# Hybrid encoder layer: last expert's down projection by quarters of its columns, second part of the last norm on TensorE for three tiles

## What is computed

```python
def expert_choice_moe(x, w_router, w_gate, w_up, w_down):
    ...
    gates, idx = lax.top_k(jnp.swapaxes(affinity, 1, 2), cap)      # cap = 64 tokens for each expert
    xe = jax.vmap(lambda xb, ib: xb[ib])(x, idx)
    hid = jax.nn.silu(xe @ w_gate) * (xe @ w_up)                   # 64 x 2048, for each expert
    ye = (hid @ w_down) * gates                                    # 64 x 1024
    # ye's rows are added to the rows idx of a (512, 1024) array of zeros
x = layer_norm(DN_ALPHA * x + expert_choice_moe(x, ...), ln3_g, ln3_b)
```

## Time and profile before

| what | us |
|---|---|
| median of 3 runs | 1263.48 (1261.69 to 1265.07) |
| the profiled execution | 1265.04 |
| its span in the profile | 1263.2 |
| TensorE busy in the span | 1171.1 (93%) |
| VectorE, ScalarE, GpSimd busy | 269.1, 192.6, 138.5 |
| read from memory | 442.02 MB, 352 GB/s over the span |
| mean granted clock of TensorE | 0.984 |

### The profile page before, as it was taken

The page is one execution under the profiler, slowest core; times in us unless marked ns, Lnnn a source line. Parts: engine busy times, 40 slices in busy tenths (PEclk is TensorE's granted clock), DMA queues, the critical chain, the costliest instruction groups (busy, mean ns, idle before and its releaser), DMA issues.

```text
span 1263.2 us, 13663 instructions
## 1 busy us (share of the span) xinstructions
PE 1171.1 (93%) x5804; PEld 590.9 (47%) x5804; DVE 269.1 (21%) x491; ACT 192.6 (15%) x348; POOL 138.5 (11%) x67
## 2 busy tenths in 40 slices
PE   8999998999999999998899889978997998899995
PEld 6887776888743433442243324323432432243321
DVE  2032377727700010010001000200110020002114
ACT  4244434143000000010000001000000000000002
POOL 4454335330000200000000000000000000000002
PEclk9999999999999999999999999999999999899998
DMA  9432213149789999999999999999999999999995
GB/s 361 183 134 83 93 67 126 40 196 386 283 309 428 433 410 431 426 436 432 432 432 432 432 432 432 432 432 431 432 432 432 432 432 432 432 423 427 429 425 210
DMA packets 28644, 444.65 MB, mean 352 GB/s; under 512 B 4544, under 2 KB 4928, under 8 KB 10304
## 3 DMA queue, kind: packets, MB, share of 16 engines
q1 hardware_dynamic: 26304, 441.89, 83.1%
q10 hardware_dynamic: 2304, 2.24, 0.5%
HBM read 442.02 MB, written 2.10 MB: 352 GB/s over the span
## 4 chain that ended last, share of the span: by engine, by line
PE 65%; DMA 28%; DVE 4%; ACT 1%; issue 1%; POOL 0%; SPq 0%; DVEq 0%; ACTq 0%; POOLq 0%
DMA ring<-in_w_exp 27%; PE bank L1293 18%; PE bank L1338 15%; PE bank L1166 5%; PE bank L1255 4%; PE bank L811 2%; PE bank L813 2%; PE bank L816 2%; PE bank L1225 1%; PE bank L989 1%; PE bank L991 1%; PE bank L990 1%; PE bank L1322 1%; DVE yt L1384 1%; PE bank L800 1%
## 5 line engine op out<-in xcount | busy, mean ns | idle before, releaser
L1293 PE MATMUL bank<-ring,yt 128*64 128x512 f32 x2000 | 451.8, 605 | 45.5 <-DMA ring<-in_w_exp 45.4
L1293 PEld LDWEIGHTS bank<-ring,yt 128*64 128x64 f32 x2000 | 145.8, 139 | 340.3 <-issue 293.1
L1338 PE MATMUL bank<-ring,yt 128*64 128x512 f32 x944 | 212.6, 603 | 21.5 <-DMA ring<-in_w_exp 16.6
L1338 PEld LDWEIGHTS bank<-ring,yt 128*64 128x64 f32 x944 | 67.8, 138 | 145.3 <-issue 128.8
L1685 DVE TENSOR_TENSOR work<-bank,work 128x512 f32<-128x512 f32 x32 | 22.1, 692 | 379.2 <-PE bank L1293 379.2
L761 ACT ACTIVATE work<-bank 128x512 f32<-128x512 f32 x32 | 19.1, 597 | 502.3 <-PE bank L1293 502.3
L547 POOL TENSOR_TENSOR stat<-stat 128x1 f32<-128x1 f32 x4 | 2.2, 553 | 831.3 <-DVE stat L1718 831.1
L532 POOL TENSOR_TENSOR piece<-ring,piece 128x1024 fp32r<-128x1024 f32 x31 | 74.7, 2410 | 97.8 <-ACT piece L598 97.8
L1696 DVE TENSOR_TENSOR xT<-bank,xT 128x512 f32<-128x512 f32 x56 | 38.8, 692 | 137.1 <-PE bank L1255 137.1
L1166 PE MATMUL bank<-yt,res 128*128 128x128 f32 x512 | 60.6, 277 | 0.0
L1166 PEld LDWEIGHTS bank<-yt,res 128*128 128x128 f32 x512 | 59.3, 194 | 0.8 <-issue 0.8
(11 more groups left out here) (247 smaller groups left out, 1083.5 us busy)
## 6 DMA issues: line engine op xcount, KB each, us to landing
ring<-in_w_exp SPq DMA_DIRECT2D x66, 4096.0 KB, 29.9
ring<-in_w_exp SPq DMA_DIRECT2D x39, 2048.0 KB, 28.6
ring<-in_dense SPq DMA_DIRECT2D x12, 2048.0 KB, 7.8
ring<-in_w_exp SPq DMA_DIRECT2D x6, 3072.0 KB, 29.1
ring<-in_w_exp SPq DMA_DIRECT2D x14, 1024.0 KB, 28.0
ring<-in_x_turned SPq DMA_DIRECT2D x8, 256.0 KB, 6.9
res<-in_na_bias SPq DMA_DIRECT2D x1, 2048.0 KB, 24.0
res<-in_x SPq DMA_DIRECT2D x1, 2048.0 KB, 7.8
```

Source lines behind the costliest of these rows:

```text
L1293: mm = nc.tensor.matmul(bank[2 * g + n % 2][64 * c:64 * c + 64, :], xeT[:, kk, 64 * e:64 * e + 64], exp_rhs(j, first, k, c), start=kk == 0 ...
L1338: mm = nc.tensor.matmul(bank[5][64 * n:64 * n + 64, :], hidT[:, s, 64 * c:64 * c + 64], exp_rhs(j, first, s, n), start=(g, c, s) == (0, 0, ...
```

## The change

The last expert's down weights are laid out otherwise by the host: chunk 20 + q holds quarter `q` (256 columns) of all 2048 hidden channels, in place of a quarter of the hidden channels for all columns. So each quarter of the output is finished with its chunk. Even and odd blocks of hidden channels go to the two partition halves and are summed by the scatter, whose matrix has the expert in both halves. ScalarE copies each finished quarter; TensorE scatters quarters 0 to 2 to banks 6 and 7 while the next chunks run, and VectorE adds them to `y_acc` and takes their statistics. Of the identity products only that of the last quarter is left. The last quarter is added in banks 0 and 1; VectorE takes its statistics, and does the gain of all four tiles in the order 0, 1, 2, 3. For tiles 0, 1 and 2 the second part of the norm is done by TensorE, with a matmul by a diagonal matrix of the inverse deviations (`scaler`, made by ScalarE) added to a product of a row of ones and the bias row; ScalarE copies the result to SBUF. Tile 3's is done by VectorE. GpSimd has only the four powers. The stores go in the order 0, 1, 2, 3.

```diff
+QUARTERS, QUARTER = 4, D // 4
+QUARTER_BANK = (5, 2, 3, 5)
+TURNED_TILES = (0, 1, 2)
+TURNED_BANKS = (3, 1, 2)
...
-            for n, t in enumerate(STORE_ORDER):
-                sp.wait_ge(normed, 2 * TT + n + 1)
+            for t in range(TT):
+                sp.wait_ge(finished[t], 2 if t in TURNED_TILES else 1)
                 sp.dma_start(out[0, P * t:P * t + P, :], y_acc[:, t, :]).then_inc(stored, 16)
...
+            for q in range(QUARTERS):
+                act.wait_ge(exp_used, LAST * CPP + (CPE + 8 + q + 1))
+                if q >= 2:
+                    act.wait_ge(last_mixed, TT + 2 * (q - 2) + 2)
+                nc.scalar.activation(y_quarter[q % 2], bank[QUARTER_BANK[q]][:, 0:QUARTER], ACT.Copy).then_inc(last_ye, 1)
+            def finish(n):
+                t = TURNED_TILES[n]
+                for a in range(2):
+                    act.wait_ge(tile_scaled, 2 * n + a + 1)
+                    nc.scalar.activation(y_acc[:, t, 512 * a:512 * a + 512], two[TURNED_BANKS[n]][:, a, :], ACT.Copy)\
+                        .then_inc(finished[t], 1)
+            for n, t in enumerate(TURNED_TILES):
+                act.wait_ge(last_rstd[t], 1)
+                nc.scalar.activation(scaler[n], ident, ACT.Copy, scale=rstd(t)).then_inc(scaler_ready, 1)
+                if n:
+                    finish(n - 1)
+            finish(len(TURNED_TILES) - 1)
...
+            def quarter_scatter(q):
+                pe.wait_ge(last_ye, 2 + q)
+                for t in range(TT):
+                    b, final = t // 2, q == QUARTERS - 1
+                    if t % 2 == 0 and not final:
+                        pe.wait_ge(last_kept, 2 * TT + (2 * (q - 1) + b + 1 if q else 0))
+                    mm = nc.tensor.matmul(in_bank(b if final else 6 + b)[:, t % 2, :], last_scat[1][:, t, :], y_quarter[q % 2],
+                                          start=not final, stop=not final or t % 2 == 1)
+                    if t % 2:
+                        mm.then_inc(tile_done if final else last_mixed, 1)
+            def quarter_down(q, ms):
+                j = CPE + 8 + q
+                for m in ms:
...
+                    for s in range(4):
+                        n = s % 2
+                        mm = nc.tensor.matmul(bank[QUARTER_BANK[q]][64 * n:64 * n + 64, 0:QUARTER],
+                                              last_hidT[m // 2][:, s, 64 * (m % 2):64 * (m % 2) + 64],
+                                              exp_chunk(j, False)[:, m, QUARTER * s:QUARTER * s + QUARTER],
+                                              start=m == 0 and s < 2, stop=m == 3 and s >= 2)
...
             def last_down():
-                turn_hid(0)
-                start_tile(1)
-                pe.wait_ge(hidT_kept, done + 1)
-                down(0, 0)
+                quarter_down(0, (0, 1))
                 turn_hid(1)
-                start_tile(2)
-                down(0, 1)
-                pe.wait_ge(hidT_kept, done + 2)
-                down(1, 0)
-                down(1, 1)
-                start_tile(3, (0,))
+                pe.wait_ge(last_kept, 2 * TT)
+                for b in range(2):
+                    nc.tensor.matmul(in_bank(b), ident, tiles_quarter(b, QUARTERS - 1), start=True, stop=False)
+                quarter_down(0, (2, 3))
+                quarter_down(1, (0, 1))
+                quarter_scatter(0)
+                quarter_down(1, (2, 3))
+                quarter_down(2, (0, 1))
+                quarter_scatter(1)
+                quarter_down(2, (2, 3))
                 pe.wait_ge(last_ye, 2)
-                for t in range(TT):
-                    if t == TT - 1:
-                        start_tile(t, (1,))
-                    last_scatter(1, t, [bank[2 * TILE_BANKS[t] + n] for n in range(2)], start=False).then_inc(tile_done, 1)
+                quarter_down(3, (0, 1))
+                quarter_scatter(2)
+                quarter_down(3, (2,))
+                quarter_down(3, (3,))
+                quarter_scatter(3)
+                pe.wait_ge(ln_in, 32 * 3)
+                pe.wait_ge(last_kept, 2 * TT + 2 * (QUARTERS - 1))
+                for n in range(len(TURNED_TILES)):
+                    for a in range(2):
+                        r = 32 * ((2 * n + a) % 3)
+                        nc.tensor.matmul(two[TURNED_BANKS[n]][:, a, :], cst[r:r + 1, C_ONE:C_ONE + P],
+                                         ln[r:r + 1, 1, 512 * a:512 * a + 512], start=True, stop=False)
+                for n, t in enumerate(TURNED_TILES):
+                    pe.wait_ge(scaler_ready, n + 1)
+                    pe.wait_ge(last_gained, t + 1)
+                    for a in range(2):
+                        nc.tensor.matmul(two[TURNED_BANKS[n]][:, a, :], scaler[n], y_acc[:, t, 512 * a:512 * a + 512],
+                                         start=False, stop=True).then_inc(tile_scaled, 1)
...
                             if last and j == CPE + 5:
-                                pe.wait_ge(last_kept, 2 * TT)
-                                start_tile(0)
+                                turn_hid(0)
...
+                    for q in range(QUARTERS - 1):
+                        for b in range(2):
+                            dve.wait_ge(last_mixed, TT + 2 * q + b + 1)
+                            y = tiles_quarter(b, q)
+                            nc.vector.tensor_tensor(y, in_bank(6 + b), y, ALU.add).then_inc(last_kept, 1)
+                            dve.wait_ge(last_kept, 2 * TT + 2 * q + b + 1)
+                            for t in (2 * b, 2 * b + 1):
+                                nc.vector.bn_stats(sums_of[t][:, 6 * q:6 * q + 6], y_acc[:, t, QUARTER * q:QUARTER * q + QUARTER])
...
+            def last_stats(t):
+                dve.wait_ge(tile_done, t // 2 + 1)
+                q = QUARTERS - 1
+                link(nc.vector.bn_stats(sums_of[t][:, 6 * q:6 * q + 6], in_bank(t // 2)[:, t % 2, :]))
+                link(nc.vector.bn_aggr(mv_of(t), sums_of[t]))
+                nc.vector.tensor_scalar(last_var(t), mv_of(t)[:, 1:2], EPS, None, ALU.add).then_inc(last_var_ready, 1)
+            def last_gain(t):
+                at = D - QUARTER
+                nc.vector.scalar_tensor_tensor(y_acc[:, t, 0:at], y_acc[:, t, 0:at], mv_of(t)[:, 0:1], ln[:, 0, 0:at],
+                                               ALU.subtract, ALU.mult)
+                nc.vector.scalar_tensor_tensor(y_acc[:, t, at:D], in_bank(t // 2)[:, t % 2, :], mv_of(t)[:, 0:1],
+                                               ln[:, 0, at:D], ALU.subtract, ALU.mult).then_inc(last_gained, 1)
+            last_stats(0)
+            last_stats(1)
             dve.wait_ge(ln_in, 32 * 3)
...
+            last_gain(0)
+            last_stats(2)
+            last_gain(1)
+            last_stats(3)
+            last_gain(2)
+            t = TT - 1
+            last_gain(t)
+            dve.wait_ge(last_gained, TT)
+            dve.wait_ge(last_rstd[t], 1)
+            row = y_acc[:, t, :]
+            nc.vector.scalar_tensor_tensor(row, row, rstd(t), ln[:, 1, :], ALU.mult, ALU.add).then_inc(finished[t], 1)
...
     out[:, 8:] = down[0].reshape(E, 4, 4, P, D).transpose(0, 1, 3, 2, 4)
+    last = down[0][E - 1].reshape(4, 4, P, QUARTERS, QUARTER).transpose(3, 2, 0, 1, 4)
+    out[E - 1, 8:] = last.reshape(QUARTERS, P, 4, 1024)
```

More of the change, by code:

```diff
@@ L240, in last_var, with tiles_quarter, in_bank @@
             return stat[:, 60 + t:61 + t]
[L242 to L251, removed]
+        def tiles_quarter(b, q):
+            return y_acc[:, 2 * b:2 * b + 2, QUARTER * q:QUARTER * q + QUARTER]
+        def in_bank(b):
+            return bank[b][:, :].rearrange("p (t n) -> p t n", t=2)
         lmax = stat[:, 32:36]
@@ L1191, in turn_scat, with last_scatter @@
                 mm.then_inc(scat_turned, 1)
-            def last_scatter(e, t, to, start):
+            def last_scatter(t):
                 for n in range(2):
                     h = slice(64 * n, 64 * n + 64)
[L1196 to L1203, removed]
@@ new lines, in last_scatter @@
+                    mm = nc.tensor.matmul(pv[n], last_scat[0][h, t, :], last_y[h, :], start=True, stop=True)
+                mm.then_inc(last_mixed, 1)
+            def quarter_scatter(q):
+                pe.wait_ge(last_ye, 2 + q)
+                for t in range(TT):
+                    b, final = t // 2, q == QUARTERS - 1
[5 more added lines that the diff above has]
+                        mm.then_inc(tile_done if final else last_mixed, 1)
@@ new lines, in turn_hid @@
+            def turn_hid(g):
+                pe.wait_ge(hid_ready, 4 * LAST + 2 + g + 1)
+                if g:
+                    pe.wait_ge(hidT_kept, 4 * LAST + 2 + g)
+                for s in range(4):
+                    mm = nc.tensor.transpose(bank[4][:, P * s:P * s + P], hid[g][:, P * s:P * s + P], ident)
+                mm.then_inc(hid_turned, 1)
+            def quarter_down(q, ms):
+                j = CPE + 8 + q
+                for m in ms:
```

(11 more changed lines are left out.)

109 lines of the change are left out of this document (25 added, 84 removed).

## The result

| | kernel before | changed kernel |
|---|---|---|
| median | 1263.48 us (1261.69 to 1265.07, 5 runs) | 1267.57 us (1265.99 to 1267.91, 5 runs) |
| ratio | 1 | 1.0026 (1.0015 to 1.0036) |
| profiled execution, its span | 1265.04, 1263.2 | 1266.91, 1265.1 |
| chunk 19's start | 1221.98 | 1221.30 |
| down's end, after chunk 19's start | 22.3 | 27.7 |

The forecast was +2.0 us, 1265.5, in a range from 1262.0 to 1268.8. The time lies in the range and the change within 0.3%, as the likeliest case had it; the ratio's interval reaches a little past 0.3% on the slow side. The ratio is an estimate over all timed executions, not the quotient of the two medians; these lie 4.09 us apart, 1.0032, twice the forecast's difference.

A forecast was written before the change was run, and what follows sets the result against it. TensorE bounds after chunk 20's landing until down's end at 1248.7, then VectorE until 1260.5, then two stores together: span 1265.2 against 1263.2, +2.0 us on the median 1263.48, so 1265.5; range 1262.0 to 1268.8.

The forecast's parts named there:

- the likeliest case: Whole kernel: a change of less than 0.3% (3.8 us) either way, given a chance of 0.78.
- The stream: TensorE's work up to down's end: 1248.7 against 1244.28 now, with chunk 19 ending as now.
- the scatter's: TensorE between the last chunks: each quarter scatter 8 instructions of 0.213, 1.71 us; three are 5.13.
- four restarts of 0.17: TensorE after chunk 20's landing: four restarts of the 64-column pattern at 0.17 (3.58 - 3.41), 0.7 us.
- Weight loads: Down chunks: twice as many loads cost 0; rival, loads in the open, +9.0 us at most, chance 0.04.
- From down's end to the last scatter: Last quarter's copy before its scatter: 0.05 + 0.38 + 0.40 after down's end at 1248.7, last scatter starting at 1249.55.
- 0.05 + 0.34 around it: Waits around ScalarE's 384 ns copy of the last quarter; the start sum has 0.05 before and 0.40 behind.
- 4.5 us of identity products: TensorE before down's end: 4.5 us of identity products became 1.7, but 5.1 of scatters came in.
- VectorE's chain: Norm after the last scatter: statistics 3.1, gains 5.4, tile 3's multiply-add 0.1 + 1.28; 9.85 us in all, ending 1260.5.
- The six one-row products: TensorE after the last scatter: 1.9 us, ready at 1253.3; rival, one after another, +3.9 us, chance 0.06.
- Stores together: Span's end: tile 3's store issued behind tile 2's, 512 KB taking 1.27 us; second lands 1264.65, span ends 1265.2.
- The clock: Rival: TensorE falls to 1.2 GHz in three tiles' products; +2.9 us in all with one tile hit, chance 0.19.

The follow-up runs named there:

- e3: Changed kernel with the scatters of quarters 0 to 2 cut to 32 of 256 columns; 1264.47 us, 1.0005 of the kernel before.
- e5: Changed kernel with tile 2 stored in two halves of 256 KB, the first as soon as ScalarE has copied it; 1265.94 us, 1.0014 of the kernel before.
- e0: The changed kernel again, no edit, timed beside the kernel before; 1267.55 us, ratio 1.0033.
- e10: The changed kernel a third time, for TensorE's clock; trace only: 35.30 us from down's first instruction to ScalarE's last copy.
- e2: Changed kernel with the norm's second part back on VectorE for all four tiles; 1268.75 us, 1.0044 of the kernel before.
- e7: Kernel before with TensorE and ScalarE finishing the norm of tiles 0 and 2, GpSimd only powers, stores in order; 1262.2 us, 0.9987 of the kernel before.
- e8: Kernel before with the edits of e6 and e7 together; 1261.23 us, 0.9972 of the kernel before.
- e1: Changed kernel with the last quarter's two identity products moved behind chunk 18, into a wait; 1266.42 us, 1.0020 of the kernel before.
- e6: Kernel before with only tile 1's identity products moved from behind chunk 19 to behind chunk 16; 1263.33 us, 0.9991 of the kernel before.
- e11: Changed kernel without the six one-row products, a repeat of e4; trace only: 35.30 us from down's first instruction to ScalarE's last copy.
- e4: Changed kernel without the six products of ones by the bias row; 1268.0 us, 1.0027 of the kernel before.

## Why the prediction was right, and where it was off

- **What bounds.** Right: TensorE from chunk 20 on (e3 moved the end one for one), VectorE behind it, the stores at the end.
- **The size.** The time was in the range, but +2.0 us was too small: +2.6 in the traces without a fall of the clock, +3.3 by the ratio, +4.1 by the medians. The terms below show where.
- **The stream, +4.4 us forecast, +5.4 measured** from chunk 19. The term that was too small is the scatter's: 8 instructions at 0.213, 1.71; measured 1.92 for each of three, 0.6 in all. e3 shows a floor under it: eight loads of 128 columns with 32 streamed take 1.01, 0.126 each. The half chunks around them cost 0.3 more than four restarts of 0.17. The wait for chunk 20 was right.
- **Weight loads.** Right: twice as many under 256 columns cost nothing, 3.60 for 32 instructions. The rule of the Trainium skill (TensorE: Matmul & The Clock Gate, "What overlaps and what doesn't") would have made that up to 9 us longer. The same page of the Trainium skill, in "Part 2: What happens when you issue a matmul", also names the background weight buffer as a case in which loads go ahead of running matmuls; that would agree with this row, though no run here shows the buffer itself.
- **From down's end to the last scatter, 0.83 forecast, 0.46 measured.** The step that failed is "0.05 + 0.34 around it" (0.40 in the sum). I read the 0.34 between ScalarE's copy and the scatter as the wait's own cost. The chain of before has an identity product of 1.06 us between down's end at 1244.28 and the scatter at 1245.34 (half of tile 3): TensorE was busy, not waiting, and 1.06 of the "4.5 us of identity products" lay behind down's end, not before it. After, a copy of 0.39 is followed by the scatter in 0.05.
- **VectorE's chain, 9.85 forecast, 10.0 measured**; 0.42, 1.01 and 0.477 us for the three new shapes, against 0.42, 1.01 and 0.475.
- **The six one-row products** ran three wide: 1.99 us for twelve instructions, where I took 1.9. One after another they would take an estimated 5.1 (12 at 0.427), 2.6 times as long. That agrees in kind with "Part 3: Packing small matmuls" on that page of the Trainium skill, which has 3.07 for four row groups.
- **Stores together.** Right: 4.4 us behind the last copy; e5's trace gets 0.6 back.
- **The clock.** Right that it can fall there, and right as a price (0.9 forecast for one tile, 0.83 measured). The chance of 0.19 was too small by these traces: it came in three of the five of the changed kernel's whole tail (the first profile and e5 without, e0, e1 and e10 with it), and in e3. The prediction names the clock at 0.50 before tile 2's products as a sign that it is wrong; the first profile doesn't show it, e0 and e10 do. What decides stays open: it came and stayed away with the one-row products and without them, which fits the prediction's suspicion that such products don't hold the clock, but doesn't show it. One row was also misread: the clock of the kernel before fell at about 1253.2, not 1253.6, since 0.57 is a mean over a microsecond that began at 1.00.
- **From +2.6 to the measured time.** With a fall the sum is +3.4, but how many of the executions without a trace had one is not known. The time outside the span adds about 0.55 us in e0's executions (2.36 against 1.81 in the medians). The forecast has no term for it. How the rest of the medians' +4.1 divides is not shown.
- **The other side.** The forecast's own sum, corrected by +1.0 in the stream and -0.4 at down's end, gives +2.6.

The two halves of the change by themselves, as ratios to the kernel before: the quarters without the norm's part on TensorE (e2) 1.0044, the norm's part without the quarters (e7) 0.9987, both together 1.0026 (the result) and 1.0033 (e0). The idea behind the quarters, less to scatter and to sum after the last weights, needs TensorE to be idle in the stream. It was idle before chunk 20 and not behind it: in the first profile the DMA share falls from 0.93 in the microsecond from 1240 to 0.28 in that from 1242, about 7 us before TensorE is through with the weights at 1249.03.

## What to carry to other kernels

Work brought forward from the tail is only free where the engine that does it waits; look for the last wait on a transfer in the chain, and put it before that (in e8 one moved identity product, the second part of two tiles' norm on TensorE and one multiply less on GpSimd make the kernel 0.28% faster), not behind. Expect a part of the gain to go to the next wait: in e1 and e6 a copy of ScalarE's, no longer covered, took back about half. When an idle interval on an engine is measured as latency, check in the chain whether another instruction filled it. Two stores that become ready together are worth splitting: in e5's trace that gave 0.6 us, which the timing was too coarse to show.

## What was not expected of the hardware

- TensorE's granted clock fell to 0.50 after short waits between matmuls, in tails where it had idled 0.48 and 0.46 us and run one-row products of 1.99 us in between (e0, e1, e3, e10). With the same pauses it held in the first profile and in e5. After 2.38 us of idling it fell in e11 and held in e4. It was back at 1.00 within the three tiles' products each time. What decides in a given execution stays open.
- GpSimd's power of one column took 0.57 us while VectorE read PSUM, and 1.25 us when it was issued just behind the start of VectorE's gain from SBUF. It cost nothing here: ScalarE waited for it (1.10 us before tile 1's `scaler`), but the chain of waits doesn't go through it:

```profile
1251.66 0.57 POOL L545 TENSOR_TENSOR stat<-stat 128x1 f32<-128x1 f32 x1 [834.37 <-DVE stat L1750]
...
1252.32 1.01 DVE L1754 SCALAR_TENSOR_TENSOR xT<-xT,stat,ln 128x768 f32<-128x768 f32 x1
...
1252.48 1.25 POOL L545 TENSOR_TENSOR stat<-stat 128x1 f32<-128x1 f32 x1 [0.25 <-DVE stat L1750]
```
